# Down projection of a feed-forward block by seven block products in place of eight

## The reference, cut to what matters

```
up, gate parts = h @ w_up                      # w_up: 1024 x 5632, 2 x 2816 features
u = causal_conv3(...)  for both parts          # per feature, over tokens
f = (conv_b part + bias) * silu(conv_a part + bias)    # 2816 features x 1024 tokens
y = f^T @ w_down                               # w_down: 2816 x 1024
out = x + rms_norm(y) * w_post
```

## Time and profile before

| | us |
|---|---|
| median of three runs (lowest, highest) | 2387.25 (2386.51, 2390.12) |
| the profiled execution's own time | 2386.57 |
| its span from first to last instruction | 2384.8 |
| PE busy in the span | 2317.7 (97%) |
| DVE busy | 1259.8 (53%) |
| ACT busy | 1063.5 (45%) |
| POOL busy | 601.8 (25%) |

### The profile page before, as it was taken

The page is one execution under the profiler, slowest core; times in us unless marked ns, Lnnn a source line. Parts: engine busy times, 40 slices in busy tenths (PEclk is TensorE's granted clock), DMA queues, the critical chain, the costliest instruction groups (busy, mean ns, idle before and its releaser), DMA issues. The chain is left out here.

```text
span 2384.8 us, 33134 instructions
## 1 busy us (share of the span) xinstructions
PE 2317.7 (97%) x12824; PEld 1890.1 (79%) x12824; DVE 1259.8 (53%) x1772; ACT 1063.5 (45%) x2262; POOL 601.8 (25%) x415
## 2 busy tenths in 40 slices
PE   7999999899999999999999999999999999999999
PEld 4887787778887787778888887677888888888887
DVE  5955205875544502795550466550787777774121
ACT  5444333773535323684434454553653333334221
POOL 2200110332310021132421130112214444465130
PEclk9999999999999999999999999999999999999999
DMA  7432110113212120103211100003222222237231
GB/s 255 150 125 71 36 53 1 37 49 128 71 47 88 36 71 18 36 1 124 89 53 30 58 1 10 19 10 140 98 81 80 80 80 88 90 133 250 86 132 45
DMA packets 139073, 181.87 MB, mean 76 GB/s; under 512 B 8700, under 2 KB 102307, under 8 KB 138917
## 3 DMA queue, kind: packets, MB, share of 16 engines
q1 hardware_dynamic: 137877, 179.74, 22.2%
q10 hardware_dynamic: 1040, 0.00, 0.0%
HBM read 151.41 MB, written 28.31 MB: 75 GB/s over the span
## 5 line engine op out<-in xcount | busy, mean ns | idle before, releaser
L856 PE MATMUL ps<-w_hi,hT_hi 128*128 128x512 f32 (+1 forms) x384 | 142.2, 370 | 2.1 <-PEq L4649 1.0
L856 PE MATMUL ps<-w_lo,hT_hi 128*128 128x512 f32 (+1 forms) x384 | 142.1, 370 | 0.0
L856 PE MATMUL ps<-w_hi,hT_lo 128*128 128x512 f32 (+1 forms) x384 | 142.1, 370 | 0.0
L856 PE MATMUL ps<-hT_hi,w_hi 128*128 128x512 f32 x360 | 140.5, 390 | 0.0
L4139 POOL TENSOR_TENSOR w_lo<-ffn_sums,w_hi 128x512 fp32r<-128x512 f32 x76 | 96.8, 1298 | 171.8 <-ACT w_hi L4321 171.8
L856 PE MATMUL ps<-hT_lo,w_hi 128*128 128x512 f32 x360 | 140.1, 389 | 0.0
L787 POOL TENSOR_TENSOR w_lo<-difp_raw,w_hi 128x2048 fp32r<-128x2048 f32 x8 | 36.8, 4604 | 386.0 <-ACT w_hi L756 386.0
L856 PE MATMUL ps<-hT_hi,w_lo 128*128 128x512 f32 x328 | 127.7, 389 | 0.0
L4189 PE MATMUL ps<-ffn_t_hi,w_hi 128*128 128x512 f32 x304 | 118.4, 389 | 0.7 <-DVE ffn_u L4498 0.7
L4189 PE MATMUL ps<-ffn_t_hi,w_lo 128*128 128x512 f32 x304 | 118.3, 389 | 0.0
L4189 PE MATMUL ps<-ffn_t_lo,w_hi 128*128 128x512 f32 x304 | 118.3, 389 | 0.0
(11 more groups left out here) (576 smaller groups left out, 6483.6 us busy)
## 6 DMA issues: line engine op xcount, KB each, us to landing
ffn_raw<-in_ffn_w_up SPq DMA_DIRECT2D x40, 512.0 KB, 4.6
mix_gla<-in_w_ada SPq DMA_DIRECT2D x32, 512.0 KB, 3.5
ffn_raw<-in_ffn_w_down SPq DMA_DIRECT2D x30, 512.0 KB, 4.7
xres<-big SPq DMA_DIRECT2D x24, 512.0 KB, 2.6
hid<-ffn_f SPq DMA_DIRECT2D x22, 512.0 KB, 2.6
ffn_sums<-hid SPq DMA_DIRECT2D x44, 256.0 KB, 3.8
glap_raw<-in_w_in SPq DMA_DIRECT2D x10, 1024.0 KB, 5.4
difp_raw<-in_w_in SPq DMA_DIRECT2D x10, 1024.0 KB, 5.0
```

Source lines behind the costliest of these rows:

```text
L856: mm = nc.tensor.matmul(out, l, r, start=(job.part != 1 and c == 0 and k == 0), stop=(job.evac and c == job.chunks - 1 and k == len(pairs) ...
```

## The change

The down projection is cast as a 2x2 block product: tokens in two halves of 512, features in two halves of 11 chunks (NK = 11), output columns in two halves of 512. Seven block products take the place of eight (table `DOWN`), each of 11 steps of 4 token tiles x 3 = 12 matmuls, 77 steps in all. Four operands of the seven on each side are sums or differences of blocks. They are made during the up projection and stored in two new DRAM tensors, `hsum` and `wsum`:

- `feature_sums(q)` on DVE: four operations of 128x512 between SBUF tiles for each pair of chunks; q = 0 in round 0 ahead of `feature`, q = 1 to 9 in the odd rounds 1 to 17, between c22 and c21, q = 10 after the last chunk. `store_feature_sums` writes them. The chunks are taken in the order 0, 11, 1, 12, ... (`feature_chunk`), and f gets two buffers.
- `part_sums(k)` on POOL: four dependent operations of 128x512 on the down weights, k = 0 to 10, each put behind the low part of operand 2 of the next round, that is in POOL's work of rounds 1 to 11. `load_parts` and `store_parts` (SP) bring the blocks in and write the sums.

In the down projection a left and a right operand of 256 KB are loaded for every step through five staging buffers each and a ring of 16 steps. ACT makes both high parts, POOL the left low part (and the first six right ones), DVE the other right ones. Each of two sets of four PSUM banks serves in turn; results are copied or combined into SBUF (`product_out` on ACT, `combine` on DVE) while the other set is used. In the seventh product each token tile is multiplied over all 11 chunks before the next, and its four results are added to what is kept, normalised and written one by one.

```diff
+DOWN = (("a11", "b11", 0, True), ("s2", "t2", 1, True), ("a12", "b21", 0, False), ("s3", "t3", 1, False),
+        ("s1", "t1", 0, True), ("a22", "t4", 1, False), ("s4", "b22", 0, False))
+NK = NF // 2
+NDOWN = NPROD * NK
@@ SP, one turn of the up projection's loop
             for j in range(PLAIN, NF - 1):
+                if j % 2:
+                    store_feature_sums((j - 3) // 2)
                 store(j - 1)
+                if j - PLAIN - 1 in range(NK):
+                    store_parts(j - PLAIN - 1)
                 if j + 3 < NF:
                     load(j + 3)
+                if j - PLAIN < NK:
+                    load_parts(j - PLAIN)
@@ POOL
+            def part_sums(k):
+                b11, b12, b21, b22 = (down.parts(i) for i in range(4))
+                pool.wait_ge(s_wload, 32 * (k + 1))
+                pool.tensor_tensor(b11, b12, b11, ALU.subtract).then_inc(s_wsum, 1)
+                pool.wait_ge(s_wsum, 4 * k + 1)
+                pool.tensor_tensor(b12, b22, b12, ALU.subtract).then_inc(s_wsum, 1)
+                pool.wait_ge(s_wsum, 4 * k + 2)
+                pool.tensor_tensor(b22, b22, b11, ALU.subtract).then_inc(s_wsum, 1)
+                pool.wait_ge(s_wsum, 4 * k + 3)
+                pool.tensor_tensor(b21, b21, b22, ALU.subtract).then_inc(s_wsum, 1)
             for n in range(ALLPROD):
                 low(n)
+                s, k = divmod(n, NPROD)
+                if k == 2 and s - 2 in range(NK):
+                    part_sums(s - 2)
@@ DVE
+            def feature_sums(q):
+                dve.wait_ge(s_f, 2 * q + 2)
+                if q:
+                    dve.wait_ge(s_fst, 16 * q)
+                nc.vector.tensor_tensor(s1, a21, a22, ALU.add).then_inc(s_fsum, 1)
+                nc.vector.tensor_tensor(s3, a11, a21, ALU.subtract).then_inc(s_fsum, 1)
+                dve.wait_ge(s_fsum, 4 * q + 1)
+                nc.vector.tensor_tensor(s2, s1, a11, ALU.subtract).then_inc(s_fsum, 1)
+                dve.wait_ge(s_fsum, 4 * q + 3)
+                nc.vector.tensor_tensor(s4, a12, s2, ALU.subtract).then_inc(s_fsum, 1)
@@ DVE, round s of the up projection
                 add(u_half(1, 1), u_half(1, 1), s, 2, s_c22)
+                if s % 2:
+                    feature_sums((s + 1) // 2)
                 dve.wait_ge(s_prod, NPROD * s + 6)
                 add(u_half(1, 0), u_half(1, 0), s, 1, s_c21)
@@ PE, down projection
+            for n in range(NDOWN - NK):
+                ready(n)
+                for i in range(4):
+                    if n % NK == 0:
+                        bank_free(n // NK, i)
+                    mm = step(n, i)
+                mm.then_inc(s_step, 1)
+            for i in range(4):
+                bank_free(NPROD - 1, i)
+                for n in range(NDOWN - NK, NDOWN):
+                    if i == 0:
+                        ready(n)
+                    mm = step(n, i)
+                mm.then_inc(s_fin, 1)
@@ DVE, after the last product, for each token tile
+            for i in range(4):
+                dve.wait_ge(s_fin, i + 1)
+                nc.vector.tensor_tensor(y12[:, i, :], y12[:, i, :], ps[:, down.BANKS[0][i], :], ALU.add).then_inc(s_y12, 1)
+                dve.wait_ge(s_y12, 4 + i + 1)
+                weigh(down.scaled(4 + i), y12[:, i, :], 1)
+                finish(4 + i, (y11[:, i, :], down.scaled(4 + i)), 12 + i + 1)
```

More of the change, by code:

```diff
@@ L3926, in chunk @@
[L3926 to L3960, removed]
+    SUMS = ("s1", "s2", "s3", "s4")
@@ new lines, in parts, with feature_sums, result, scaled @@
+    def parts(self, c=slice(0, 4)):
+        return self.up.m.hT_raw[:, 0, c, 512:1024]
+    def feature_sums(self, q):
+        if q == NK - 1:
+            return self.t_raw[:, 0, 3, :, :]
+        return self.up.m.hT_raw[:, 1, 0:4, 512:1024]
+    def result(self, name):
+        t, h = self.t_raw, self.up.m.hT_raw
+        return {"c21": t[:, 0, 3, :, :], "c12": t[:, 1, 3, :, :], "c22": h[:, 0, 4:8, 512:1024],
+                "c11": h[:, 1, 4:8, 512:1024]}[name]
+    def scaled(self, x):
+        return self.up.raw[:, x // 4, 512 * (x % 4):512 * (x % 4) + 512]
@@ L3966, in stage_ffn @@
+def stage_ffn(nc, m, w_up, w_down, hid, hsum, wsum, fcols, w_post, out, xres, block, opening):
     pad = FFN_K - 1
@@ L3987, in stage_ffn @@
         op = UpOperands(m, raw, sums, t_hi, t_lo)
-        down = DownOperands(op, w_down, hid)
+        down = DownOperands(op, t_raw, w_down, hid, hsum, wsum)
         halves = [slice(0, 512), slice(512, 1024)]
-        t_post, junk = [sums[:, (NWINO - 1) % 2, 2 * b:2 * b + 2, :].rearrange("p a n -> p (a n)") for b in range(2)]
-        rows = [u[:, 0, 0:D], u[:, 1, 0:D], f[:, :]]
+        y11, y12, y21, y22 = (down.result(n) for n in ("c11", "c12", "c21", "c22"))
+        rows, junk = [u[:, 0, 0:D], u[:, 1, 0:D], f[:, 0, :]], f[:, 1, 0:512]
+        tiles = [4, 5, 6, 7, 0, 1, 2, 3]
         def tap(j, k, up):
-            c = 2 * NF * k + NF * up + j
+            c = 2 * NF * k + NF * up + feature_chunk(j)
             return fcols[:, c:c + 1]
@@ L4113, in _ @@
                     sp.wait_ge(s_st, 16 * NF)
+                    sp.wait_ge(s_fst, 16 * NK)
                     load_row(2)
[L4115 to L4126, removed]
@@ L4127, in _ @@
-            i = NT - 1
+            for x in range(NT - 1):
+                store_row(x)
+                if x + 3 < NT:
+                    load_row(x + 3)
+            x = NT - 1
             for half in range(2):
-                sp.wait_ge(s_new, NT + half)
-                sp.dma_start(out[P * i:P * i + P, halves[half]], rows[i % 3][:, halves[half]]).then_inc(s_out[i % 3], 16)
+                sp.wait_ge(s_new, 2 * x + half + 1)
+                sp.dma_start(out[P * tiles[x]:P * tiles[x] + P, halves[half]],
+                             rows[x % 3][:, halves[half]]).then_inc(s_out[x % 3], 16)
@@ L4217, in winograd, with ready @@
                 product(NPROD * s + 6)
[L4219 to L4228, removed]
+            def ready(n):
+                pe.wait_ge(s_alo, n + 1)
+                if n < down.POOLED:
+                    pe.wait_ge(s_blo, n + 1)
+                else:
+                    pe.wait_ge(s_blov, n - down.POOLED + 1)
@@ L4229, in step @@
+            def step(n, i):
+                r, k = divmod(n, NK)
+                (a_hi, a_lo), (b_hi, b_lo) = down.unit(n, 0), down.unit(n, 1)
                 toks = slice(P * i, P * i + P)
-                for n, (l, r_) in enumerate(((h_hi, w_hi), (h_hi, w_lo), (h_lo, w_hi))):
-                    mm = nc.tensor.matmul(ps[:, 2 * i + half, :], l[:, toks], r_[:, half, :],
-                                          start=(k % NF == 0 and n == 0), stop=(k % NF == NF - 1 and n == 2))
-                return mm
@@ L4235, in ready @@
[L4235 to L4239, removed]
-                if n < down.POOLED:
-                    pe.wait_ge(s_wlo, n + 1)
-                else:
-                    pe.wait_ge(s_wlov, n - down.POOLED + 1)
+                for j, (l, r_) in enumerate(((a_hi, b_hi), (a_hi, b_lo), (a_lo, b_hi))):
+                    mm = nc.tensor.matmul(ps[:, down.BANKS[DOWN[r][2]][i], :], l[:, toks], r_,
+                                          start=(DOWN[r][3] and k == 0 and j == 0), stop=(k == NK - 1 and j == 2),
+                                          skip_group_check=True)
@@ new lines, in product_out, with square, first_share @@
+            def product_out(r, dst, signal):
+                act.wait_ge(s_step, NK * (r + 1))
+                for i in range(4):
+                    nc.scalar.activation(dst[:, i, :], ps[:, down.BANKS[0][i], :], ACT.Copy).then_inc(signal, 1)
+            def square(x, half, src, done):
+                i = tiles[x]
+                act.wait_ge(s_sq, done)
+                nc.scalar.activation(junk, src, ACT.Square, accum_out=ssq[:, half, i:i + 1]).then_inc(s_sq, 1)
+            def first_share(x, half, done):
+                i = tiles[x]
+                act.wait_ge(s_sq, done)
+                own.mark(nc.scalar.activation(bias[:, i:i + 1], ssq[:, half, i:i + 1], ACT.Identity,
+                                              bias=m.eps[:, 0:1], scale=1.0 / D))
```

429 lines of the change are left out of this document (262 added, 167 removed).

## The result

The changed kernel takes 2417.53 us (median of four runs, 2414.66 to 2420.28), the kernel before 2386.9 in the same job (2386.51 to 2390.12): a ratio of 1.0125, 95% interval 1.0108 to 1.0143. That is **30.6 us slower**, where +9.3 was forecast. The sign was right, the size was not: the time lies 10 us above the range.

A forecast was written before the change was run, and what follows sets the result against it. PE was taken to bound both projections, each added PE wait costing its full length. Matmuls -29.9, tail +0.8, waits +35.4 and clock +3 gave +9.3 on 2386.57, taken as 2396 us; range 2370 to 2407.

The forecast's parts named there:

- Matmuls removed: Down projection: 924 matmuls instead of 1056, 132 x 0.2267 = 29.9 us off, all on the path.
- Feeding the down projection: Down projection: loads, ACT, POOL and DVE all keep under the 2.72 us step; 0 taken, bounds 0 to 4 us.
- The bad start at step 6: Down projection: one bad start allowed at step 6 or 11, where DVE comes late; within bounds 0 to 4 us.
- DVE and POOL in turns: Up projection: DVE and POOL exclude each other at SBUF, delaying q2; PE waits sum to 35.4 us, bounds 28 to 42.
- the waits hide: Rival, up projection: POOL's part sums come when DVE does not need SBUF; 2359, chance 0.10.
- come to half: Rival, up projection: sums not separated by POOL, or shared rates; waits 17 to 27, time 2375 to 2385, chance 0.25.
- Clock: Up projection: granted clock may fall behind PE's long waits; 3 us taken, bounds 0 and 6 x 1.7 = 10.
- The catching up: Up projection: a slower PE gives DVE time, so part of the clock loss comes back; 3 us remains.
- clock and queue on top: Rival: six long waits each lower the clock (+7 over 3), part blocks or down-projection start late (+2 to 4); 2403 to 2407, chance 0.17.
- Tail: After the last matmul: one DVE addition (0.69) before ACT's square; 0.8 us more, bounds 0.5 to 1.5.

The follow-up runs named there:

- e3: Changed kernel with POOL's part sums and DVE's feature sums of q = 1 to 9 both cut to 8 columns, transfers kept: 2362.15 us (ratio 0.9898).
- e9: Changed kernel with part sums spread and after the last conv part, POOL waiting for feature sums, rows 3 to 6 buffered separately, ACT and DVE orders changed: 2374.88 us.
- e10: e9 without POOL's wait for the feature sums in odd rounds: 2385.95 us (ratio 0.9994).
- e11: e9 with POOL's wait for the feature sums one low part earlier, before the second instead of the third: 2371.87 us (ratio 0.9936).
- e5: Changed kernel with POOL's part sums moved behind the round's last conv part and their loads ahead of the weights': 2403.26 us (ratio 1.0069).
- e7: Kernel before the change with five idle DVE reductions of 1024 elements ahead of q2 in six rounds: 2428.34 us (ratio 1.0173).
- e8: Kernel before the change with three idle DVE reductions of 768 elements ahead of q2 in rounds 1 to 18: 2420.96 us (ratio 1.0146).
- e4: Changed kernel with residual rows 3 to 6 in buffers of their own, loaded ahead of all output stores: 2416.52 us (ratio 1.0126).
- e1: Changed kernel with POOL's four part sums cut from 128x512 to 128x8, loads and stores kept: 2377.60 us (ratio 0.9961).

## Why the prediction was right and wrong

- **Matmuls removed**, -29.9: measured -29.9.
- **Feeding the down projection**, 0: right. 792 matmuls in 179.53 us without a gap. The bad start at step 6 that I allowed for does come, at 0.6 to 1.7 us, in e3, e9, e10 and e11.
- **DVE and POOL in turns**, +35.4: right, as a mechanism and nearly in size. Waits behind the odd rounds 1 to 11 were 4.15, 4.70, 4.68, 4.69, 4.70 and 4.68 (forecast 3.3, then 4.4 each): 27.6 against 25.3. Behind the even rounds 2 to 10 1.57, 0.65, 1.61, 1.05 and 0.79: 5.7 against 4.5. Rounds 13 and 15 1.29 each against 1.0; the wait in round 18 grew by 2.4 against 2.2; round 0 0.86 against 1.3. Sum 39.1 against 35.4, within the bounds 28 to 42. The Trainium skill's SBUF — State Buffer, "Who interferes with whom", says that only work that needs the shared ports is locked out; the traces agree in both directions: 1776 to 1786 ns for a feature sum behind POOL, 673 to 692 for all 95 additions that read PSUM. The rivals in which the waits hide or come to half fell.
- **Clock**, +3: this is the step that failed. I took 1.7 us for each of six long waits as the bound, then under a third of it, because a slower PE "gives DVE time to catch up". Seven falls came, with 13.6 us of slow matmuls. The catching up is real, but I had no number for it, and it is partial. Where another wait follows, a longer burst shortens it. Behind the burst of 2.5 in round 4 of the change the next wait was 0.65, behind that of 1.5 in round 6 it was 1.61:

```profile
1895.32 0.50 PE L4283 MATMUL ps<-ffn_t_hi,w_hi 128*128 128x512 f32 x1 [0.65 <-DVE ffn_u L4611]
1941.84 0.50 PE L4283 MATMUL ps<-ffn_t_hi,w_hi 128*128 128x512 f32 x1 [1.61 <-DVE ffn_u L4611]
```

Both times the next long wait ended 46.5 to 46.6 us after the last one. In e5 three falls gave back all they cost. Where no wait follows, nothing comes back: not in rounds 12 and 18 of the change, and not in e7, whose rounds lasted 25.4 to 26.3, which is 19.04 and the wait, the 0.31 and the slow matmuls in full. No run has the long waits of the change without the falls, so the 13.6 is what the slow matmuls took, and how much less time the rounds would take without them is open. The rows had one fall and one twin without it behind 1.8 us; a wait more than twice as long (not three times, as I wrote in the rival) should have been taken as the likelier case. The rival "clock and queue on top" had the right mechanism and too small a price (+7 over my 3, where 10.6 came), and queue trouble that didn't come.
- **What a stop costs beyond its record**, 0: not in the sum at all. 4.3 here for 14 more waits; e8 measures 0.31 for each.
- **Tail**, +0.8 (bounds 0.5 to 1.5): mis-sized, +3.6. I looked at the last tile's arithmetic alone. The row buffers' store, load, store, 5.3 to 5.4 us a link, started at 2380.2, when the first of the eight rows was written, and ended after PE. e4 cuts 3.0 of it, and leaves 6.08 against 5.46, so the arithmetic's part was 0.6, as forecast.
- The **2.6 us** by which the rounds start earlier were not forecast; that part of the program is unchanged, and its end moves by 5.5 us over the thirteen traces.

Forecast to measured, on the span: +9.3, +10.6 slow matmuls, +4.3 beyond the record, +3.7 waits, +2.8 tail, -2.6 ahead of the rounds: +28.1. The profiled execution lies 2.9 under the median.

Left open, besides the net price of the falls: what decides whether a wait of 2.8 brings the clock down (four of ten did), and why a burst has 6 slow matmuls in one place and 14 in another.

## What to carry to other kernels

When two engines can lock each other out, count what each operation costs with the other beside it, and move the engine whose result is due later: a wait put on POOL made PE's waits shorter. Price a stall of PE by more than its recorded length: add what the trace shows for each stop and for the matmuls at half speed behind it, so one stall of 4.5 us (6.4 to 7.3 in e7) is dearer than three of 1.4 (5.2 in e8). Take the slow matmuls off again where PE would have stood for the same engine anyway, as in e5. Where buffers rotate between stores and loads, follow that chain to the end on its own; it can end after the engine that sets the pace.

## What the runs showed that was not expected

- Every recorded wait of 3.04 us or more in these rounds was followed by 7 to 14 starts 0.43 apart instead of 0.23, in all kernels that had one. Of ten waits of 2.76 to 2.82 four were (one in e1, three of six in e5, none of three in e10). Waits up to 1.8 in the rounds never were.
- A wait costs about 0.31 us more than its record says (e8, 17 rounds).
- In e5 the same kind of round took 23.85 us with a second wait and no fall of the clock, and 23.83 with the fall and no second wait.
- Two effects of 39.9 and 39.3 us, each removed alone, came to 55.4 together. Either removal took away the same six longest waits and the slow matmuls behind them.
